# Weight sums, partial results and the gate tile in PSUM, low parts of the feature sums on GpSimd

## What is computed

```
h = rms_norm(x, g)                               # x: 512 tokens x 1024 features
gate, up = jnp.split(h @ w_gate_up, 2, axis=-1)  # 1024 -> 2 x 2816
y = (jax.nn.silu(gate) * up) @ w_down            # 2816 -> 1024
```

## Time and profile before

| what | us |
|---|---|
| median of 3 runs | 2943.77 |
| lowest, highest | 2942.05, 2945.72 |
| the profiled execution's own time | 2939.47 |
| its span, first to last instruction | 2937.7 |
| PE busy (share) | 2710.1 (92%) |
| DVE busy | 1758.5 (60%) |
| POOL busy | 1588.4 (54%) |
| ACT busy | 1351.5 (46%) |
| mean granted clock of PE | 0.972 |

### The profile page before, as it was taken

The page is one execution under the profiler, slowest core; times in us unless marked ns, Lnnn a source line. Parts: engine busy times, 40 slices in busy tenths (PEclk is TensorE's granted clock), DMA queues, the critical chain, the costliest instruction groups (busy, mean ns, idle before and its releaser), DMA issues.

```text
span 2937.7 us, 46989 instructions
## 1 busy us (share of the span) xinstructions
PE 2710.1 (92%) x16306; PEld 2362.0 (80%) x16306; DVE 1758.5 (60%) x2721; ACT 1351.5 (46%) x2426; POOL 1588.4 (54%) x1033
## 2 busy tenths in 40 slices
PE   9998898989999898999999997989899999789997
PEld 7767888888867888888878876888888878688886
DVE  6775748467455757555545347484757633766664
ACT  7664434346574434343255334343447533443443
POOL 4653656664453666565446335565654453466663
PEclk9999999999999999999999998999999999899998
DMA  4301122223302222232214111222222341122312
GB/s 169 108 2 58 65 101 86 92 102 104 101 16 68 81 91 93 88 110 90 97 51 148 61 65 58 91 81 101 101 93 93 113 138 51 44 101 72 108 66 86
DMA packets 69276, 252.78 MB, mean 86 GB/s; under 512 B 7680, under 2 KB 7936, under 8 KB 68864
## 3 DMA queue, kind: packets, MB, share of 16 engines
q1 hardware_dynamic: 68112, 247.43, 24.5%
q10 hardware_dynamic: 1008, 3.28, 0.3%
HBM read 248.58 MB, written 2.10 MB: 85 GB/s over the span
## 4 chain that ended last, share of the span: by engine, by line
PE 65%; DVE 18%; issue 10%; ACT 5%; POOL 1%; DMA 1%; DVEq 0%; ACTq 0%; SPq 0%; POOLq 0%
PE ps L744 13%; PE ps L745 13%; PE ps L746 13%; PE ps L1137 5%; PE ps L1141 4%; PE ps L1139 4%; PE ps L911 3%; PE ps L949 2%; DVE w_sum L2113 2%; DVE w_sum L2108 2%; DVE tmpb L2163 2%; DVE w_lo L2125 2%; PE ps L934 1%; DVE w_sum L2111 1%; DVE tmpb L2195 1%
## 5 line engine op out<-in xcount | busy, mean ns | idle before, releaser
L625 POOL TENSOR_TENSOR w_lo<-w_raw,w_hi 128x1024 fp32r<-128x1024 f32 x300 | 731.3, 2445 | 734.3 <-ACT w_hi L1365 723.4
L671 POOL TENSOR_TENSOR w_lo<-w_raw,w_hi 128x512 fp32r<-128x512 f32 x240 | 360.8, 1519 | 204.9 <-ACT w_hi L1349 204.9
L1365 ACT ACTIVATE w_hi<-w_raw 128x1024 fp32r<-128x1024 f32 x302 | 316.8, 1055 | 308.4 <-PE ps L746 227.7
L671 POOL TENSOR_TENSOR w_lo<-w_sum,w_hi 128x512 fp32r<-128x512 f32 x240 | 332.0, 1400 | 225.1 <-ACT w_hi L1349 225.1
L744 PE MATMUL ps<-xh,w_hi 128*128 128x512 f32 x980 | 390.5, 398 | 24.6 <-DVE xl L1930 14.3
L1137 PE MATMUL ps<-xh,w_hi 128*128 128x256 f32 x960 | 289.3, 301 | 128.1 <-ACT ev L1536 120.1
L1137 PE MATMUL ps<-t_hi,w_hi 128*128 128x256 f32 x1280 | 373.2, 292 | 21.8 <-POOL w_lo L671 20.2
L745 PE MATMUL ps<-xl,w_hi 128*128 128x512 f32 x980 | 383.3, 391 | 0.0
L746 PE MATMUL ps<-xh,w_lo 128*128 128x512 f32 x980 | 383.1, 391 | 0.0
L1139 PE MATMUL ps<-t_lo,w_hi 128*128 128x256 f32 x1280 | 371.7, 290 | 0.0
L1141 PE MATMUL ps<-t_hi,w_lo 128*128 128x256 f32 x1280 | 370.5, 289 | 0.0
(11 more groups left out here) (340 smaller groups left out, 5762.8 us busy)
## 6 DMA issues: line engine op xcount, KB each, us to landing
w_raw<-weights_in SPq DMA_DIRECT2D x462, 512.0 KB, 3.3
x<-x_in SPq DMA_DIRECT2D x4, 512.0 KB, 7.8
mem<-mem_in ACTq DMA_DIRECT2D x2, 1024.0 KB, 4.8
x_out<-x SPq DMA_DIRECT2D x4, 512.0 KB, 2.6
rope<-rope_in SPq DMA_DIRECT2D x1, 512.0 KB, 10.5
tab<-tables_in ACTq DMA_DIRECT2D x2, 256.0 KB, 2.8
tab<-tables_in SPq DMA_DIRECT2D x1, 384.0 KB, 11.0
small<-small_in ACTq DMA_DIRECT2D x1, 326.5 KB, 4.9
```

The costliest lines, as they stand in the source:

```text
L625: nc.gpsimd.tensor_tensor(w_lo[:, slot], w_raw[:, slot], w_hi.bitcast(f32)[:, slot], ALU.subtract).then_inc(lo_ready, 1)
L671: last = nc.gpsimd.tensor_tensor(quad(w_lo, name, q), src, quad(w_hi, name, q).bitcast(f32), ALU.subtract)
L1365: A(w_hi[:, s], w_raw[:, s], ACT.Copy).then_inc(hi_ready, 1)
```

## The change

- `w_sum` has two tiles in SBUF (q3, q4) in place of four; the sums of q2 and q5 go to PSUM banks 4 and 5. POOL can't read them, so DVE makes the low parts of q2 and q5, and POOL those of q0, q1, q3, q4, q6.
- Pairs use banks 0 to 3 alone: b and c stay, a alternates between two.
- The sum of b and its copy, and of c and its copy, is written back into the bank and multiplied by `rstd` from there, each in an instruction of half size.
- The gate tile lives in bank 6 or 7: silu, product, `hh` and `hl` of pairs work on it there.
- ACT copies c ahead of `hidden_high` and of nothing else new; one high part (q3) goes between them.
- `combined_low` is gone from DVE; POOL does all four (`combined_lows`) ahead of the first pair's low parts. All `combine` calls are in `gate_up`, two before and two behind `rstd`; the first weight sums stand there too. The second plain tile's product and split move into the first pair.

```diff
-        EV_FIRST = 8
-        SUM_OF = {2: 0, 3: 1, 4: 2, 5: 3}
+        EV_FIRST = 12
+        SUM_OF = {3: w_sum[:, 0], 4: w_sum[:, 1], 2: ps[:, 4, :], 5: ps[:, 5, :]}
+        ADDED = {"b": 1, "up0": 2, "a": 3, "c": 4, "up1": 5, "gate0": 6}
...
         def pair_banks(name, pair):
-            if pair % 2 == 0:
-                return 4, 5, 6
             r = BANK0[name] % RING
-            return tuple((r + 1 + i) % RING for i in range(3))
+            return (r + 3 * (pair % 2)) % RING, (r + 1) % RING, (r + 2) % RING
+        def gate_bank(pair):
+            return ps[:, 6 + pair % 2, :]
...
                     for q in range(QUADS):
-                        if q == 5:
+                        if q in (2, 5):
                             continue
...
+            def combined_lows(f):
+                for k in range(4):
+                    pool.wait_ge(th_ready, 4 * f + k + 1)
+                    nc.gpsimd.tensor_tensor(t_lo[:, :, k], t_f[:, k % 2], t_hi[:, :, k].bitcast(f32),
+                                            ALU.subtract).then_inc(tl_ready, 1)
+
             def feed_forward_lows(f):
+                combined_lows(f)
...
                     ahead(2)
+                    copy_part(pair, i, 2, 3, "c")
+                    ahead(3)
                     if pair:
                         hidden_high(pair - 1, i)
-                    copy_part(pair, i, 2, 3, "c")
-                    for q in range(3, QUADS):
+                    elif part == "a":
+                        classic_high(CLASSIC - 1)
+                    for q in range(4, QUADS):
                         ahead(q)
...
+                combine(0, gname)
+                combine(1, gname)
+                if f < 2:
+                    inverse_rms(rstd, 1e-5)
+                else:
+                    inverse_rms_kept(1e-6)
+                combine(2, gname)
+                sums_of_first(first, (3, 4))
+                evict(0)
+                evict(1)
+                combine(3, gname)
+                sums_of_first(first, (2, 5))
+                n_.tl.n += 4
+                classic_product(0)
+                low_of_sum(first, 0, 2)
+                classic_low(0)
+                evict(2)
+                evict(3)
+                low_of_sum(first, 0, 5)
...
-                    added(V.tensor_tensor(up[:, first], b, ev[:, 0], ALU.add))
+                    V.tensor_tensor(b, b, ev[:, 0], ALU.add).then_inc(ev_added, 1)
                     ahead(2)
+                    added("b")
+                    V.tensor_tensor(up[:, first], b, rstd[:, first], ALU.mult).then_inc(ev_added, 1)
                     ahead(5)
                     if pair:
                         hidden_product(pair - 1, i)
-                        hidden_low(pair - 1, i)
+                    elif part == "a":
+                        classic_product(CLASSIC - 1)
                     done(4)
                     copied(2)
-                    added(V.tensor_tensor(gate[:, second], a, ev[:, 2], ALU.add))
+                    V.tensor_tensor(gate[:, second], a, ev[:, 2], ALU.add).then_inc(ev_added, 1)
+                    low_ahead(2)
+                    if pair:
+                        hidden_low(pair - 1, i)
...
-                    V.tensor_tensor(up, up, rstd[:], ALU.mult)
+                    added("c")
+                    V.tensor_tensor(up[:, second], c, rstd[:, second], ALU.mult).then_inc(ev_added, 1)
```

More of the change, by code:

```diff
@@ new lines, in bank_free @@
+                    def bank_free(bank):
+                        before = {"a": (2, "gate0"), "b": (1, "up0"), "c": (1, "up1")}[bank]
+                        pe.wait_ge(ev_added, pair_at(6 * (g - before[0]) + ADDED[before[1]] + EV_FIRST, i, 6))
+                        if pair == 0:
+                            pe.wait_ge(evac_done, BANK0[name] - {"a": 3, "b": 2, "c": 1}[bank])
+                        if pair == 1 and bank == "a":
+                            pe.wait_ge(evac_done, BANK0[name])
@@ L2117, in sum_weights, with sums_of_first @@
                 ins.then_inc(sums_ready, 1)
-            def sums_of_first(name):
-                for which in (3, 4, 2, 5):
-                    sum_weights(name, 0, which)
-            def low_of_sum(name, pair, i=None):
-                dve.wait_ge(hi_ready, pair_at(product_done(name, pair, 5), i, QUADS))
-                V.tensor_tensor(quad(w_lo, name, 5), w_sum[:, SUM_OF[5]], quad(w_hi, name, 5).bitcast(f32),
+            def sums_of_first(name, which=(3, 4, 2, 5)):
+                for q in which:
+                    sum_weights(name, 0, q)
@@ L2157, in pairs @@
                 n, j0 = PAIRS[name], CLASSIC if part == "a" else 0
-                silus, hidden = n_.silu.n, n_.hh.n
+                silus, hidden = n_.silu.n + (part == "a"), n_.hh.n + (part == "a")
                 first, second = slice(0, HALF), slice(HALF, T)
@@ L2175, in body @@
                     a, b, c = (ps[:, bank, 0:HALF] for bank in pair_banks(name, pair))
-                    up, gate = tmpb[:, pair % 2], tmpa[:, pair % 2]
+                    up, gate = tmpb[:, pair % 2], gate_bank(pair)
                     def done(q):
@@ L2521, in memory_attention @@
                 attention(UX, {})
-                copies_out(f"xo{e}", y_mid, f"pairs{2 + e}a")
+                copies_out(f"xo{e}", y_mid)
                 inverse_rms_rows(1e-6)
```

194 lines of the change are left out of this document (92 added, 102 removed).

## The result

The changed kernel took **2813.6 us** (median of 4 runs, 2811.7 to 2814.6), against 2943.2 (2942.1 to 2945.7) of the kernel before on the same chip: a ratio of 0.956, with a 95% interval from 0.954 to 0.957. That is in the range (2760 to 2838), 21 us above the forecast of 2793: 130 us were won where 150 were forecast. The span went from 2937.7 to 2811.7 us, 126.0.

A forecast was written before the change was run, and what follows sets the result against it. The prediction took PE's wait before q5 for ACT's copy of bank c as the bound. Savings of 96.0 (pairs), 25 and 28.6 us (starts), 150 off 2939.5, gave 2789.5, with 4.3 for the median 2793; range 2760 to 2838.

The forecast's parts named there:

- size of the starts: Starts and parts a, stage `gu` and first pair: -25 us for f = 0 and 1, -13.7 and -14.9 for f = 2, 3.
- The chain from `rstd` to q0: Start of part a: combines, sums, evictions, POOL's `t_lo` and quad q0 take 12 us; q0 at 308.7 in f = 0.
- Steady pair: Parts b and c: 10.6 us for every pair but the last (10.3), 591.2 against 687.2 us, -96.0.
- The copy of c now stands behind the q2 high part alone: ACT in the steady pair: the copy could start at 346.76 in place of 348.19, 1.4 us of PE's 2.2 us wait.
- up (0.34), q5 sum: DVE's work after the q2 sum at 6.6 us; with the rest it ends at 10.7, 0.1 to 0.2 in hand.
- First pair of b as the model for all: Part b's first pair before the change, 10.6 us with PE idle 0.33, taken for every pair but a part's last.
- Which instructions queue: DVE behind POOL: only q3, q4, q2 sums, with two SBUF operands, queue: first two near 1.8 us, q2 at 1.4.
- slower: Rival, 3%: a PSUM operand does not spare DVE the queue behind POOL; 13.5 us a pair, 2968 us.
- the rule weighed in the forecast: DVE instructions with a PSUM source cost 65 ns more; some 18 us in all, time 2811.
- DVE becomes the bound: Rival, 22%: DVE's reserve is 0.1 to 0.2 us; up to 0.9 us in 64 pairs, 58 us: 2851; half, 2822.
- PE never waits: Rival, 12%: DVE goes before POOL, the q4 sum ends 1.2 us earlier; pairs of 10.3, 2774 us.
- What the forecast said bounds the kernel before: Pairs: PE stands before q5 until ACT has copied bank c, 2.24 us; stretches lose 188 us against an unhindered PE.

## Why the prediction was right or wrong

- **Direction right; size of the starts right in sum, by luck in part.** Starts and parts a gave -50.4 in place of -53.6; 4.0 more came outside them, where the forecast had counted nothing. The shares are others too: counted from the part before, f = 0 and 1 ended part a 7.9 and 10.1 us earlier, where 12.6 each were forecast. In f = 0 q0 came at 311.8, not 308.7, and PE waited 7.45 us for POOL, not 4. The chain from `rstd` to q0 is 12.2 us (299.6 to 311.8, and 1712.5 to 1724.65), as forecast (12); `rstd` itself was 3 us late: DVE's last feature sum ahead of it queued behind POOL's `t_lo`, and ACT's second `t_hi` stood ahead of the root, as these rows show. In f = 2 and 3 the wait for POOL was 9.45 as forecast (9), and each gave 16.2 where 13.7 and 14.9 were forecast; the first pair took 13.0 us, with the clock after the wait in it, where 12.5 and 2.6 for the clock were forecast.

```profile
290.15 2.63 DVE L2116 SCALAR_TENSOR_TENSOR t_f<-x,small,t_f 128x256 f32<-128x256 f32 x1
292.81 1.06 ACT L1514 ACTIVATE t_hi<-t_f 128x1024 fp32r<-128x1024 f32 x1 [2.39 <-DVE t_f L2116]
```

- **Steady pair: the term that failed.** "The copy of c now stands behind the q2 high part alone" is true of ACT's queue and wrong for its time: that high part waits for the q5 sum. The term "up (0.34), q5 sum" stood in the forecast's DVE sum, but behind the q2 sum's release, not before it. It costs 0.45 us of PE's wait (0.78 against 0.33): b and c fell short by 24.4, which is 0.5 in each of their 48 pairs that aren't the last of a part.
- **First pair of b as the model for all.** It was taken over with its release; in the changed kernel that pair itself takes 11.2, not 10.6. With the release of before (the q2 sum in SBUF) it takes 10.6 again.
- **Which instructions queue: right.** L2132 and L2135 take 1.67 and 1.81, L2137 1.45, as forecast (1.8, 1.8, 1.4). What has an operand in PSUM does not: of the 160 low parts below 19 start inside a POOL instruction, of the 80 `hl<-ps,hh` 68, and none takes over 0.70. DVE's groups between 312 and 2765 (count | busy us, mean ns of one):

```profile
L2137 DVE SCALAR_TENSOR_TENSOR ps<-w_sum,w_raw 128x512 f32<-128x512 f32 x79 | 115.2, 1458 | 0.0
L2149 DVE TENSOR_TENSOR w_lo<-ps,w_hi 128x512 fp32r<-128x512 f32 x160 | 108.4, 682 | 4.7 <-ACT w_hi L1368 4.7
L2140 DVE TENSOR_TENSOR ps<-w_raw,ps 128x512 f32<-128x512 f32 x79 | 53.8, 682 | 0.4
```

  This settles the rival "slower", whose open point was subtractions into `w_lo`: 160 of them at 0.682. It settles the rule weighed in the forecast as well: an instruction with a PSUM source takes 0.682, and one with both in SBUF and no POOL in its way 0.68, so the 65 ns more of the Trainium skill's page "VectorE: DVE Perf Modes", section on the TRN2 errata, are not there, and neither are its 18 us.
- **"DVE becomes the bound" (22%): not in the changed kernel.** It keeps pace even with pairs of 10.1 once PE isn't held up. "PE never waits" (12%) came only in three pairs of f = 2, by the turn that it named; what decides it in all pairs is what stands ahead of ACT's copy.
- **What the forecast said bounds the kernel before** ("PE stands before q5 until ACT has copied bank c") was the last wait, not the only one. Had that been all, the order alone had brought 110 us, and it brought 20.6 (42.4 in the pairs that aren't the last of a part). The sum came near since the change moved both walls.
- **The range.** Its upper end, 2838, is called two thirds of the price of a DVE bound; it is 45 us above the forecast, over three quarters of the 58. Nothing hangs on it.
